# Two constant products in front of each wait for the probabilities, in the attention of a hybrid decoder trunk

## The reference

```python
logits = jnp.einsum("bqhd,bkhd->bhqk", qi, k).astype(jnp.float32) * scale
logits = jnp.where(kpos[None, :] <= qpos[:, None], logits, -jnp.inf)
pr = jax.nn.softmax(logits, axis=-1).astype(v.dtype)
return jnp.einsum("bhqk,bkhd->bqhd", pr, v)
```

## Time and profile before

| | |
|---|---|
| median of 3 runs | 1611.13 us (1608.15 to 1614.7) |
| profiled execution, time | 1612.89 us |
| its span, first to last instruction | 1611.2 us |
| TensorE busy | 1359.9 us, 84% |
| VectorE busy | 1102.4 us, 68% |
| ScalarE busy | 720.4 us, 45% |
| granted clock of TensorE, mean of the span | 0.898 of full speed |
| attention, per layer | 91.6 us |
| granted clock of TensorE there | 0.78 |

### The profile page before, as it was taken

How to read it: one execution, slowest core, us unless ns; L and a number is a source line. 1 busy time by engine, 2 the same in 40 slices (tenths; PEclk the granted TensorE clock), 3 DMA queues, 4 the chain that set the end, 5 groups by cost and what they waited for, 6 DMA issues and landing times. The chain is left out here.

```text
span 1611.2 us, 16817 instructions
## 1 busy us (share of the span) xinstructions
PE 1359.9 (84%) x6187; PEld 1051.9 (65%) x6187; DVE 1102.4 (68%) x1315; ACT 720.4 (45%) x975; POOL 186.6 (12%) x268
## 2 busy tenths in 40 slices
PE   7599987987849999999718998888794899999981
PEld 3377785656637777777506777666573777777761
DVE  0677764674558888888458786566556788888862
ACT  1423433453317766666223333345412566666640
POOL 0000014400100100000020000261010000010002
PEclk9699999688959999999858999978796899999995
DMA  9536561330538999998364374243125699999944
GB/s 342 197 107 250 168 227 53 131 108 37 225 127 328 404 406 395 395 404 328 118 225 175 130 274 161 97 152 105 66 96 229 259 386 398 401 408 401 392 149 169
DMA packets 95259, 379.52 MB, mean 236 GB/s; under 512 B 5897, under 2 KB 8695, under 8 KB 85704
## 3 DMA queue, kind: packets, MB, share of 16 engines
q1 hardware_dynamic: 71592, 308.82, 50.8%
q0 software_dynamic: 15264, 55.63, 8.9%
q10 hardware_dynamic: 8320, 13.96, 2.5%
HBM read 345.58 MB, written 32.82 MB: 235 GB/s over the span
## 5 line engine op out<-in xcount | busy, mean ns | idle before, releaser
L1022 PE MATMUL ps<-mod_rounded,work_rounded 128*128 128x512 f32 x340 | 139.7, 411 | 3.9 <-DVE work_rounded L1821 3.9
L1024 PE MATMUL ps<-mod_rounded,work_rounded 128*128 128x512 f32 x340 | 135.7, 399 | 0.0
L1705 DVE TENSOR_TENSOR ring_rounded<-ring,mod_rounded 128x2048 fp32r<-128x2048 f32 (+1 forms) x54 | 102.6, 1930 | 33.8 <-ACT mod_rounded L1311 33.8
L1705 DVE TENSOR_TENSOR work_rounded<-work,mod_rounded 128x2048 fp32r<-128x2048 f32 (+1 forms) x48 | 91.3, 1930 | 37.0 <-ACT mod_rounded L1311 37.0
L1023 PE MATMUL ps<-ring_rounded,work_rounded 128*128 128x512 f32 x288 | 114.6, 398 | 0.0
L1398 DVE SCALAR_TENSOR_TENSOR gain<-ring,csil,gain 128x512 f32<-128x512 f32 x134 | 101.8, 760 | 4.5 <-DMA ring<-in_ada_w 1.4
L1023 PE MATMUL ps<-work_rounded 128*128 128x512 f32 x256 | 101.3, 396 | 0.0
L779 PE MATMUL ps<-ring_rounded,actT_rounded 128*128 128x512 f32 (+1 forms) x256 | 93.5, 365 | 0.0
L1311 ACT ACTIVATE mod_rounded<-ring 128x2048 fp32r<-128x2048 f32 (+1 forms) x54 | 86.0, 1631 | 0.0
L1106 ACT ACTIVATE work<-x 128x1024 f32<-128x1024 f32 x16 | 16.9, 1059 | 153.7 <-DVE x L1421 80.1
L1174 ACT ACTIVATE work<-ps 128x512 f32<-128x512 f32 (+1 forms) x48 | 26.3, 549 | 129.5 <-PE ps L779 77.7
(11 more groups left out here) (325 smaller groups left out, 3546.5 us busy)
## 6 DMA issues: line engine op xcount, KB each, us to landing
ring<-in_ada_w SPq DMA_DIRECT2D x38, 1024.0 KB, 5.8
ring<-in_moe_w_gate SPq DMA_DIRECT2D x18, 2048.0 KB, 10.1
ring<-in_moe_w_up SPq DMA_DIRECT2D x18, 2048.0 KB, 10.4
ring<-in_moe_w_down SPq DMA_DIRECT2D x18, 2048.0 KB, 11.5
work<-in_moe_w_gate SPq DMA_DIRECT2D x16, 2048.0 KB, 10.1
work<-in_moe_w_up SPq DMA_DIRECT2D x16, 2048.0 KB, 10.8
work<-in_moe_w_down SPq DMA_DIRECT2D x16, 2048.0 KB, 11.5
expert_rows<-work POOLq DMA_DIRECT2D x34, 512.0 KB, 8.1
```

Of the source, the lines that this page charges most:

```text
L1022: pe.matmul(ps[j][:, :], xl, hi, start=k == 0, stop=False)
L1024: mm = pe.matmul(ps[j][:, :], xh, hi, start=False, stop=k == KD - 1)
L1705: v.tensor_tensor(slots_r[3 * odd + j][:, 512 * k0:512 * k1], slots[3 * odd + j][:, 512 * k0:512 * k1], buf.bitcast(F32), ALU.subtract).th ...
```

## The change

A function `fill(n)` is added and called in each of the 32 steps, behind `scores(n + 2)` and ahead of `turn_p(n)`, whose first instruction waits for `p_dn`. It multiplies the identity by itself, twice, in f32, into columns 256 to 383 of the bank of head (n - 1) // 4. Nothing reads these columns. When the bank passes to a new head (from the third on), `fill` first waits until the head that had it before is out, as `pv` does.

```diff
+                def fill(n):
+
+                    h = max(n - 1, 0) // T
+                    if n >= 1 and (n - 1) % T == 0 and h >= 2:
+                        pe.wait_ge(o_dn, h - 1)
+                    for _ in range(2):
+                        pe.matmul(ps[6 + h % 2][:, 256:256 + P], ident, ident, start=True, stop=True)
+
...
                     if n + 2 < 8 * T:
                         scores(n + 2)
+                    fill(n)
                     turn_p(n)
                     if n > 0:
                         pv(n - 1)
```

## The result

The changed kernel takes 1636.55 us (median of 4, 1630.27 to 1640.39) against 1611.11: a ratio of 1.0153, interval 1.0113 to 1.0193. It is slower by 25 us where 9 us of gain were forecast, and slower than the dearest rival (1622).

The account below looks back on a forecast made before the run. Attention was taken as bound by VectorE at full clock and TensorE at half clock. Per layer, -7.3 us from the clock and +2.7 for pairs gave -4.6, or -9.2 over two layers: 1602 us, own range 1597 to 1607, with rivals 1592 to 1620.

Parts of the forecast that it names:

- the dearest rival: Attention stage: all pairs run in series and TensorE becomes the bound; 1622 us, chance 0.13.
- The two regimes: Attention stage: at half clock TensorE sets the pace, at full clock VectorE does; 41.0 us at half clock.
- A pair at full clock, 0.45 us: Six VectorE waits a layer, five before `q_out`, one before a division: one pair exposed at each, costing 2.7 us.
- rival 4: Attention stage: all pairs in series, TensorE becomes the bound; +11.5 us, 1622 us, chance 0.13.
- A pair at half clock, 0.86 us: `fill` on TensorE's queue: a pair of constant products takes 0.86 us at 1.2 GHz.
- part 4: Attention clock: falls at 301.5, 325.4 and 349.3 go, first half-clock stretch at least halves; worth 7.3 us a layer.
- Denser at half clock, so the first stretch is halved: Attention after 281.1: pairs fill TensorE's short gaps, cutting the 13.6 us half-clock stretch to half or less.
- Rival 3: Attention: clock falls as before, four boundaries hold a pair at 0.86 us, two at 0.45; +8.7 us, 1620, chance 0.12.
- The size of what the clock is worth: Attention stage: clock gain of 7.3 us less pair cost of 2.7 us, net -4.6 us a layer.
- rival 1: Attention: TensorE's pace counts between the waits too; -8.8 us a layer, -17.6 in all, 1593 us, chance 0.15.
- Transposes and the clock: `turn_p` and `turn_qk`: transposes taken to count for the clock as products do, since 1.00 followed 32 transposes.

Follow-up runs that it names:

- e2_late: The changed kernel with its pairs of products only in steps 16 to 31 of each layer; 1613.31 us, 0.9992 of the kernel before.
- e9_cover6: The changed kernel, two products a step kept, plus six further products ahead of the scores of step 6; 1593.79 us, 0.9874 of the kernel before.
- e8_four32: The changed kernel with four products a step instead of two, over 32 rows of the identity instead of 128; 1714.89 us, 1.0602 of the kernel before.
- e3_early: The changed kernel with its pairs of products only in steps 0 to 15 of each layer; 1626.15 us, 1.0082 of the kernel before.
- e4_four: The changed kernel with four full products a step instead of two; 1610.30 us, 0.9978 of the kernel before.
- e5_cover: The changed kernel plus six further products ahead of the scores of steps 6 and 27; 1594.32 us, 0.9873 of the kernel before.

## Why the prediction was wrong

- *The two regimes* (full clock: VectorE sets the pace; half clock: TensorE): right. The stage's VectorE time stayed at 60.65 us in 100.7, and the half-clock heads carry the loss.
- *A pair at full clock, 0.45 us, one in each head on the path*: right, if anything too dear. The waits at `q_out` are 2.17 and 2.59, forecast 2.56. Heads with pairs take 9.4 us, and TensorE is busy 27.68 of 30.70 us at full clock. In the sixth head it is 9.27 of 9.45, a share I had called a sign of rival 4, but that head is no longer than before; so rival 4, which is as near by its number (1622), had the wrong mechanism.
- *A pair at half clock, 0.86 us*: the price was 0.10 us too low (0.96 by e2_late against the change), but it stood in the sum only as a rival's four places. At half clock all four of a head are in series. The nine of the long stretch (steps 6 to 14) make 8.6 us, about the whole growth of the stage (9.1).
- *The clock* (part 4): this is the step that failed. Its term was -7.3 us a layer, for three falls gone and the first stretch halved; the runs show 40.9 us at half clock, before 41.0, so nothing was won, and the pairs in it had to be paid. I read the pauses out of the trace of before and asked whether a pair lies in them. But that trace showed only the pauses of a TensorE that was at half clock for 13.6 us just there. With the pairs of the first steps the clock held past 281 (the pause there is 0.94 us now, before 1.81), TensorE then did step 5 at full speed and came 2.28 us early to a wait that VectorE's squares had always held (0.39 us of it showed before), ahead of the scores, where no pair stands. Six products in that pause and nothing else (e9_cover6) turn 1636.55 into 1593.79 us. I had the squares in the earlier trace rows as "VectorE busy 10.63 of 13.60" and took it as cover that makes a slow TensorE free; it was also the pause of a fast one.
- *"Denser at half clock, so the first stretch is halved"*: wrong. TensorE is shown busy 37.50 of 37.50 us there and stayed at half clock. Busy by this profile is no sign that the clock will rise; e8_four32 has it busy 146.91 of 147.15 at a mean of 0.62.
- *Rival 3* (the clock falls as before, pairs cost at half clock, 1620) had the nearest mechanism, but not the new place of the fall, and only four half-clock pairs a layer in it, where the long stretch has nine.
- *The size of what the clock is worth*: -8.5 us a layer with the clock held (83.1 against 91.6), pairs included. I had -4.6, rival 1 -8.8. Rival 1's mechanism, TensorE's pace between the waits too, was the better sum; that it comes so near is partly luck, for it takes off 2.7 us for pairs that hardly show at full clock.
- *Transposes and the clock*: the Trainium skill, "TensorE: Matmul & The Clock Gate", section "PE-mode transpose", says that a transpose doesn't count as TensorE being busy in the way a matmul does. That was the ground of rival 3. The runs here don't separate transposes from products; the earlier trace rows stays the only evidence, against that sentence. Its clock is 1.00 from 1154.9 on, and the last of the 32 transposes ends at 1155.6, so it rose while they still ran.
- *Two readings were loose*, without weight for the outcome: the two stages of the earlier trace rows agree within 0.12 us and not to a hundredth (VectorE 60.31 and 60.19), and of the wait of 6.24 us ahead of 319.98 the last 1.4 us lie behind the clock's rise at 318.6.

What remains of the 25 us beside the stage: 18.2 us of the span are the two attentions, and 3.3 us lie elsewhere in the profiled execution. 1.1 of these are the piece right behind the first attention, 17.60 us at a clock of 0.52 where before it was 16.50 at 0.69. The medians differ by 4 us more than the spans; with e3_early's 1424.8 us outside the attention against 1431.3 here, that part varies between executions by more than this. Why a stretch once begun lasts 37.5 us in the changed kernel and 3.4 to 17.1 in the trace of the kernel before is not settled. The pairs alone don't explain the length, since e2_late had 54.6 us without any. The runs show what prevents the stretch, not what would end it.

## What to carry to other kernels

Look for the pauses in which work added to hold TensorE's clock would have to stand, and also for the one that appears only once TensorE is fast; a trace taken at half clock doesn't show it, so look at what the other engines do there. In this kernel such work was free where VectorE set the pace at full clock, and was paid in full at half clock: with one pause left open it was a loss (1636.55 us), and six products more in that pause made it a gain (1593.79 us). More work in every step kept the clock too, but cost as much as it gave (four a step, 1610.30 us). Compare stretches cut at the clock's changes, never the stage's mean clock.

## What the runs showed of the hardware

- The same four 128-column products a step take 1.15 us over 32 rows and 1.16 over 128, but with the former the stage had 113 and 117 us at half clock (e8_four32) and with the latter none (e4_four). The part of the array that works matters, not only the time for which TensorE is occupied.
- A product of the identity with itself, nearly all zeros, holds the clock: nothing but such products was added in e4_four, e5_cover and e9_cover6, and all half clock in the stage went.
- TensorE can be shown busy without a break and stay at half clock: 37.50 of 37.50 us at 0.50 in the change, 13.89 of 13.89 us without any constant product in e2_late.
- The clock fell behind single pauses of 1.36 to 2.46 us, but not behind each of that length: it fell behind the 1.74 us at step 27 in the change and stayed at 1.00 behind the 1.74 us there in e9_cover6.
